# Token rows gathered as quarter rows and turned by VectorE instead of TensorE in a mixture-of-experts kernel

## The reference

```python
v = rms_norm(h, norm2_g).reshape(B * S, D)
h = h + moe(v, router_w, router_b, w1, b1, w2, b2).reshape(B, S, D)
# moe: logits = xf @ router_w + router_b; top_val, top_idx = lax.top_k(logits, 4) of 32 experts
#      gates = softmax(top_val)
def clamped_swiglu_expert(xb, w1, b1, w2, b2):        # for each expert, its tokens only
    h = xb @ w1 + b1                                  # 1024 -> 2 * 1024
    x_glu = jnp.minimum(h[..., :D_FF], 7.0)
    x_lin = jnp.clip(h[..., D_FF:], -7.0, 7.0)
    act = x_glu * jax.nn.sigmoid(1.702 * x_glu) * (x_lin + 1.0)
    return act @ w2 + b2                              # 1024 -> 1024, times the gate, added to the token's row
```

## Time and profile before

| | |
|---|---|
| median of 3 runs | 2027.03 us (2025.29 to 2027.17) |
| the profiled execution's own time | 2026.22 us |
| its span in the trace | 2024.4 us |
| mean granted TensorE clock | 0.985 of full speed |
| PE busy | 1956.3 us, 97% of the span |
| DVE busy | 992.1 us, 49% |
| POOL busy | 228.0 us, 11% |
| HBM traffic | 251 GB/s over the span |

### The profile page before, as it was taken

The page is one execution under the profiler, slowest core; times in us unless marked ns, Lnnn a source line. Parts: engine busy times, 40 slices in busy tenths (PEclk is TensorE's granted clock), DMA queues, the critical chain, the costliest instruction groups (busy, mean ns, idle before and its releaser), DMA issues.

```text
span 2024.4 us, 35446 instructions
## 1 busy us (share of the span) xinstructions
PE 1956.3 (97%) x13245; PEld 1620.3 (80%) x13246; DVE 992.1 (49%) x2418; ACT 451.5 (22%) x983; POOL 228.0 (11%) x221
## 2 busy tenths in 40 slices
PE   6999989969999999999999999999999999999996
PEld 3555544437888877888887888999999999999996
DVE  3998963354455545454454555444444433343332
ACT  3166564111111111111111111221222211111111
POOL 3111100010101100110100010111111111100100
PEclk9999989989999999999999999999999999999998
DMA  6000123537999999998999998998888888887651
GB/s 238 1 1 1 46 59 139 175 131 276 346 321 330 345 334 344 345 335 317 345 334 344 343 339 309 311 315 299 295 295 298 296 301 298 289 284 245 217 174 43
DMA packets 233939, 509.08 MB, mean 251 GB/s; under 512 B 7997, under 2 KB 12633, under 8 KB 233888
## 3 DMA queue, kind: packets, MB, share of 16 engines
q1 hardware_dynamic: 215264, 447.97, 61.2%
q0 software_dynamic: 16768, 59.98, 11.1%
q10 hardware_dynamic: 1856, 0.41, 0.1%
HBM read 475.53 MB, written 32.80 MB: 251 GB/s over the span
## 4 chain that ended last, share of the span: by engine, by line
PE 93%; DVE 3%; ACT 1%; issue 1%; POOL 1%; DMA 0%; SPq 0%; ACTq 0%; DVEq 0%; POOLq 0%
PE bank L1133 49%; PE bank L1173 12%; PE bank L1148 11%; PE bank L1366 6%; PE bank L1244 5%; PE bank L1513 2%; PE bank L1280 2%; DVE arena L874 2%; PE bank L1291 1%; PE bank L1317 1%; PE bank L1161 1%; PE bank L1504 1%; PE bank L1162 1%; DMA arena<-in_x 0%; PE bank L1340 0%
## 5 line engine op out<-in xcount | busy, mean ns | idle before, releaser
L1133 PE MATMUL bank<-arena 128*128 128x128 f32 (+5 forms) x8192 | 993.6, 283 | 6.9 <-DVE arena L1099 5.6
L1133 PEld LDWEIGHTS bank<-arena 128*128 128x128 f32 x8192 | 984.5, 191 | 18.3 <-issue 9.3
L769 DVE TENSOR_SCALAR arena<-bank,b1c 128x256 f32<-128x256 f32 x256 | 123.6, 483 | 424.3 <-PE bank L1133 424.3
L469 ACT ACTIVATE arena<-arena 128x256 f32<-128x256 f32 x256 | 106.6, 417 | 853.3 <-DVE arena L769 853.3
L1099 DVE TENSOR_SCALAR arena<-bank,cols 128x256 f32<-128x256 f32 x256 | 112.0, 479 | 337.0 <-PE bank L1513 337.0
L1173 PE MATMUL bank<-arena 128*128 128x512 f32 x576 | 262.1, 593 | 0.0
L1148 PE MATMUL bank<-arena 128*128 128x144 f32 (+4 forms) x1792 | 246.0, 293 | 0.0
L1148 PEld LDWEIGHTS bank<-arena 128*128 128x128 f32 x1792 | 235.9, 190 | 0.1
L357 POOL DMA_INDIRECT out<-arena,idx_cur x64 | 99.0, 1547 | 873.3 <-DVE arena L817 863.6
L874 DVE SCALAR_TENSOR_TENSOR arena<-arena,cols 128x512 f32<-128x512 f32 (+1 forms) x226 | 182.2, 806 | 16.3 <-ACT arena L562 9.4
L1173 PEld LDWEIGHTS bank<-arena 128*128 128x128 f32 x576 | 102.5, 190 | 94.7 <-issue 94.7
(11 more groups left out here) (226 smaller groups left out, 1107.9 us busy)
## 6 DMA issues: line engine op xcount, KB each, us to landing
arena<-in_w SPq DMA_DIRECT2D x192, 2048.0 KB, 11.4
arena<-in_b SPq DMA_DIRECT2D x32, 512.0 KB, 11.0
arena<-in_x SPq DMA_DIRECT2D x16, 512.0 KB, 6.2
token_rows<-arena SPq DMA_DIRECT2D x8, 528.0 KB, 2.9
out<-arena SPq DMA_DIRECT2D x8, 512.0 KB, 5.9
arena<-in_w_in SPq DMA_DIRECT2D x2, 1536.0 KB, 13.7
arena<-in_w_in SPq DMA_DIRECT2D x1, 3072.0 KB, 20.1
arena<-in_w_out SPq DMA_DIRECT2D x1, 2048.0 KB, 8.2
```

The costliest lines, as they stand in the source:

```text
L469: a.activation(sg[:, m % 2, :], g1[:, m % 2, :], ACT.Sigmoid, scale=ALPHA).then_inc(sg_ready, 1)
L769: v.tensor_scalar(g1[:, r, :], bank[r][:, 0:SLOTS], b1c[:, m:m + 1], LIMIT, ALU.add, ALU.min).then_inc(g1_ready, 1)
L1133: last = mm(bank[m % 2][:, side * SLOTS:side * SLOTS + n], w1_sb[:, k, lo:lo + P], xT[:, k, 0:n], start=k == 0, stop=k == KD - 1)
```

## The change

The gathered data no longer comes as whole rows. `token_rows` holds rows with the gain already multiplied in and with their values in another order: the four quarters of each 128-value block are collected, so that quarter q of a row is 256 contiguous values. POOL gathers eight lists of 128 quarter rows (1 KB each): list g brings tokens 32g to 32g+31, with quarter q of them on partitions 32q to 32q+31. A VectorE transpose of 32x32 blocks then writes 32 columns of `xT` directly. The gates have an HBM scratch of their own and two gathers of 128-byte rows. The indices of the eight lists need one more small matmul (`spots` spread over the partitions by `copies`). `slots_to_tokens` moves from behind group 3 to behind group 2. The first pass still goes by two gathers and PE transposes, with a reordering copy on ACT ahead. The end of the router loop is written in another order too.

```diff
-        def gather(pool, n):
-            pool.wait_ge(idx_ready, n)
+        def gather_gates(pool):
+            for h in range(2):
+                pool.indirect_dma_start(out=gsel[:, h, :], out_offset=None, in_=gates_d,
...
+        def gather_quads(pool, n):
+            pool.wait_ge(idx_q_ready, n)
+            pool.sem_inc(pool_past, 1)
+            for g in range(8):
+                pool.indirect_dma_start(out=gath_q[:, g, :], out_offset=None, in_=quads_d,
+                                        in_offset=bass.IndirectOffsetOnAxis(ap=idx_q[:, g:g + 1], axis=0)
+                                        ).then_inc(quad_in, 16)
...
                 pool.wait_ge(cur_ready, q + 1)
-                pool.wait_ge(xt_mm, q * 4 + 4)
-                gather(pool, q + 2)
+                pool.wait_ge(xt_ev, q * 4 + 4)
+                gather_quads(pool, q + 1)
+                gather_gates(pool)
                 pool.wait_ge(y_ready, q + 1)
...
-                if m == 4:
                     v.wait_ge(idx_mm, q + 2)
-                    first, second = take_idx()
-                    link(first)
-                    second().then_inc(idx_ready, 1)
+                    link(take_codes(v))
+                    link(take_idx(v, idxf[:]))
+                    v.tensor_copy(idx_next[:], idxf[:]).then_inc(idx_ready, 1)
+                    v.tensor_tensor(spots[:], idxf[:].unsqueeze(2).to_broadcast([P, 2, 4]),
+                                    quad[:].unsqueeze(1).to_broadcast([P, 2, 4]), ALU.mult).then_inc(spots_ready, 1)
+                if m == 5:
+                    v.wait_ge(spread_mm, q + 1)
+                    v.tensor_scalar(idx_q[:], bank[6][:, 16:24], 4.0, quad_id[:], ALU.mult, ALU.add
+                                    ).then_inc(idx_q_ready, 1)
             hidden_b(MT - 1)
-            q4 = v.snap(q * 4 + 4)
-            for i in range(4):
-                take_xT(q4, i)
+            v.wait_ge(quad_in, q * 128 + 128)
+            for g in range(8):
+                ins = v.transpose(xT[:, :, g * 32:(g + 1) * 32], gath_q[:, g, :].rearrange("p (k r) -> p k r", k=KD))
+                if g % 2 == 1:
+                    ins.then_inc(xt_ev, 1)
...
             def norm_v(t):
-                v.tensor_scalar(vrow[:, t % 2, 0:D], hb[:, t % 4, :], rs[:, 2, t:t + 1], None, ALU.mult)
+                for g in range(4):
+                    v.scalar_tensor_tensor(dst[:, g], src[:, g], rs[:, 2, t:t + 1], gain[:, g], ALU.mult, ALU.mult)
...
+            residual(NT - 1, (0,))
+            route(NT - 2)
+            residual(NT - 1, (1,))
+            v.wait_ge(lt_mm, NT - 1)
+            v.wait_ge(vt_mm, 2 * NT)
+            v.tensor_copy(vT[:, 4:8, :], bank[5][:].rearrange("p (k q) -> p k q", k=4)).then_inc(vt_ev, 1)
+            norm_v(NT - 1)
+            route(NT - 1)
...
-                        if m == 0 and side == 0 and k % 2 == 0:
-                            pe.wait_ge(xt_ev, q4 - 3 + k // 2)
+                        if m == 0 and side == 0 and k == 0:
+                            pe.wait_ge(xt_ev, q4)
...
-                if m == 3:
+                if m == 2:
                     slots_to_tokens(q + 2)
+                if m == 4:
+                    pe.wait_ge(spots_ready, q + 1)
+                    mm(bank[6][:, 16:24], copies[:], spots[:].rearrange("p h g -> p (h g)"), start=True,
+                       stop=True).then_inc(spread_mm, 1)
...
             if n == P:
-                down_rows(0, range(4))
-                for h in range(2):
-                    pe.wait_ge(gath_in[h], q16 + 16)
-                pe.wait_ge(idx_ready, q + 2)
-                trans_x(q4, 0, halves)
...
+                down_rows(0, range(MT))
+                down_rows(1, range(MT))
                 return
```

More of the change, by code:

```diff
@@ L179, in hybrid_block @@
         gate_cur = sb("gate_cur", [P, 2])
+        gsel = sb("gsel", [P, 2, NE])
+        idxf = sb("idxf", [P, 2])
+        spots = sb("spots", [P, 2, 4])
+        idx_q = sb("idx_q", [P, 8], i32)
+        copies = sb("copies", [P, P])
+        quad = sb("quad", [P, 4])
+        quad_id = sb("quad_id", [P, 1])
         lnv = sb("lnv", [P, 2, NT // 2])
@@ L689, in h_square, with take_vT @@
                              ).then_inc(h_sq, 1)
-            def take_vT(t):
+            def take_vT(t, sides=(0, 1)):
                 if t >= 1:
                     a.wait_ge(lt_mm, t)
-                for b in range(2):
+                for b in sides:
                     a.wait_ge(vt_mm, 2 * t + b + 1)
@@ L725, in _ @@
             take_lT(NT - 1)
[L726 to L729 removed]
             gate_exp(NT - 1)
+            a.wait_ge(h_sq, NT)
+            for h in range(2):
+                a.wait_ge(gath_in[h], 16)
+                a.activation(first_tok[:, h, :].rearrange("p (k q r) -> p q k r", k=KD, q=4),
+                             gath[:, h, :].rearrange("p (q k r) -> p q k r", k=KD, q=4), ACT.Copy
+                             ).then_inc(first_tok_ready, 1)
             for i in range(2):
@@ L955, in _, with residual @@
             softmax_a(NT - 1)
-            def residual(t):
+            def residual(t, sides=(0, 1)):
                 v.wait_ge(xh_in[t % 2], 16 * (t // 2 + 1))
@@ L1346, in weigh_v, with out_half @@
                 last.then_inc(o_mm, 1)
-            def out_half(t, part_, sides=(0, 1)):
+            def out_half(t, part_, sides=(0, 1), ins=range(CT)):
                 if part_ == 0:
@@ L1362, in out_half @@
                 for b in sides:
-                    for i in range(CT):
+                    for i in ins:
                         src = (aT if part_ == 0 else cT)[:, i, t * P:(t + 1) * P]
@@ new lines, in turn_rows @@
+            def turn_rows(u, sides=(0, 1)):
+                if u == 0:
+                    pe.wait_ge(cn_done, 2 * CT)
+                if u == 1:
+                    pe.wait_ge(o_ev, NT)
+                for b in sides:
+                    if u >= 1:
+                        pe.wait_ge(vt_ev, 2 * u)
+                    pe.wait_ge(h_ready if b else h_half, u + 1)
+                    for k in range(4):
+                        c = 4 * b + k
+                        last = pe.transpose(bank[4 + b][:, k * P:(k + 1) * P], hb[:, u % 4, c * P:(c + 1) * P], ident[:])
+                    last.then_inc(vt_mm, 1)
@@ new lines, in logits @@
+            def logits(u):
+                pe.wait_ge(vt_ev, 2 * u + 2)
+                if u >= 1:
+                    pe.wait_ge(lg_neg, u)
+                for j in range(2):
+                    for g in range(4):
+                        last = mm(bank[6][g * NE:(g + 1) * NE, 0:P], rw[:, 4 * j + g, :], vT[:, 4 * j + g, :],
+                                  start=j == 0, stop=j == 1)
+                last.then_inc(lt_mm, 1)
+            for t in range(NT - 1):
+                if t >= 2:
+                    out_half(t, 0)
+                if t >= 1:
+                    turn_rows(t - 1)
+                if t >= 2:
+                    fold_logits(t - 2)
+                if t == 0:
+                    pe.wait_ge(mix_ready, CT)
+                if t == NT // 2:
+                    pe.wait_ge(mix_ready, 2 * CT)
+                out_half(t, 1)
@@ L1469, in _ @@
                     out_half(1, 0, (1,))
-                if 1 <= t <= NT:
-                    u = t - 1
-                    pe.wait_ge(vt_ev, 2 * u + 2)
-                    if u >= 1:
-                        pe.wait_ge(lg_neg, u)
-                    for j in range(2):
-                        for g in range(4):
-                            last = mm(bank[6][g * NE:(g + 1) * NE, 0:P], rw[:, 4 * j + g, :], vT[:, 4 * j + g, :],
-                                      start=j == 0, stop=j == 1)
-                    last.then_inc(lt_mm, 1)
+                else:
+                    logits(t - 1)
                 if t == 1:
@@ L1482, in _ @@
                     weigh_v(NT - 1)
+            out_half(NT - 1, 0)
+            turn_rows(NT - 2)
+            fold_logits(NT - 3)
+            out_half(NT - 1, 1, (0,))
+            logits(NT - 2)
+            out_half(NT - 1, 1, (1,), range(2))
+            turn_rows(NT - 1, (0,))
+            fold_logits(NT - 2)
+            out_half(NT - 1, 1, (1,), range(2, CT))
+            turn_rows(NT - 1, (1,))
+            logits(NT - 1)
             fold_logits(NT - 1)
@@ L1506, in slots_to_tokens @@
                 last.then_inc(idx_mm, 1)
-            def trans_x(before, i, halves=2):
-                if i >= 1:
-                    pe.wait_ge(xt_ev, before + i)
-                for k in (2 * i, 2 * i + 1):
-                    for h in range(halves):
-                        last = pe.transpose(bank[6][:, (k % 2) * SLOTS + h * P:(k % 2) * SLOTS + (h + 1) * P],
-                                            gath[:, h, k * P:(k + 1) * P], ident[:])
-                last.then_inc(xt_mm, 1)
             slots_to_tokens(1)
@@ L1545, in _, with passes @@
                 lap8 = pe.snap(lap * len(WIDTHS))
```

(6 more changed lines are left out.)

169 lines of the change are left out of this document (63 added, 106 removed).

## The result

| | before | changed kernel |
|---|---|---|
| median | 2027.1 us (4 runs) | 2114.97 us (4 runs, 2114.11 to 2118.71) |
| ratio | | 1.0437 [1.0422, 1.0452] |
| span of the profiled execution | 2024.4 us | 2113.1 us |
| mean granted TensorE clock | 0.985 | 0.966 |

The change makes the kernel 88 us slower, where 25 us less were forecast.

The account below looks back on a forecast made before the run. PE was taken as the bound, busy 97% of the span and holding 93% of the chain. 2026.2 - 41.4 + 4.5 + 4.2 + 2.5 + 5 = 2001.0; with the runs' median 0.8 higher, 2001.8 us, range 1992 to 2032.

Parts of the forecast that it names:

- Wide passes: No wait: Wide passes: the next tokens' chain takes 21.3 us where 25 us are left, so PE does not wait.
- rival 1: Narrow passes: tokens come late, 2.0 us a pass (2031 us), 2068 with slow transposes; chance 0.18 beyond break-even, with rival 4.
- Transposes on PE: PE's own path in all passes: 376 row transposes of 0.11 us each go, -41.4 us.
- The spread matmul: Added on PE, once in each of 32 passes: 0.14 us each, +4.5 us, bounds 1.6 to 7.
- The wait for the one-hots: Behind group 2 of the 18 narrow passes: PE waits 0.23 us each, +4.2 us.
- The next tokens in narrow passes: At the end of narrow passes: PE waits 0.3 us for the next tokens in 17 passes, +5 us.
- The last list landed: Next tokens, narrow pass: the eighth list was forecast to land 5.8 us from issue, range 4.4 to 7.5.
- the eight transposes: VectorE, behind the last list's landing: eight transposes at a pitch of 0.42 us, 3.4 us together.
- The estimate of 0.62: One VectorE transpose: 622 ns from the skill page's 311 ns, eight 5.0 us, which would put the sum 27 us higher.
- The router loop: Ahead of the pass loop: the last block's routing starts late, at 438.1, +2.5 us.
- Rival 3: DMA becomes the bound in narrow passes: 2037 us at 0.11 us a packet; chance 0.03.
- Rival 4: VectorE holds up POOL's issues: lists 1.7 us later, wait 2.0 a pass, 2031 us; chance 0.18 together with rival 1.

Follow-up runs that it names:

- experiment 16: The changed kernel with one semaphore count-up on POOL between its eighth list and its gates, nothing else: 2019.46 us, 0.9967.
- 13: The changed kernel with one-hots behind the first group's evictions and one semaphore count-up on POOL between the eighth list and the gates: 2011.82 us, 0.9926.
- experiment 8: The kernel before with eight plain loads per pass by SP, the same bytes as eight extra gathers: 2026.68 us, 1.0002.
- experiments 12 to 14: Changed kernel, one-hots early, plus before the gates a wait with count-up (2008.32 us) or count-up alone (2011.82), or a count-up between the gates' two gathers (2009.64).
- 10 to 15 and 18: Changed kernel, one-hots early, with gates gathered first (10, 11, 15) or a wait or count-up among the last issues (12 to 14, 18): 2008.32 to 2011.82 us.
- experiment 2: The changed kernel with DVE's one-hots written behind the first group's evictions instead of the second's: 2107.87 us, 1.0403.

## Why the prediction was wrong, step by step

- **The step that failed** is "Wide passes: No wait", and with it rival 1's remark that ten issues in a row have no precedent, which it priced only as a late landing. The lists did land in time. What came was a mechanism that neither the sum nor a rival has: the ten issues in a row held ACT, which PE needs for the next column group. By the last column of the table against the second it cost 90.0 us in 13 wide passes, 2.8 in passes 1 to 18, 1.8 in the last and 1.1 behind it: 95.6 of span, 95.5 by the medians (2114.97 - 2019.46). In the pass shown, 5.80 us of idle PE stand against 0.23 in the timeline of 16, and the slow clock takes 2.0 on the first 16 records (4.21 for 2.23), 0.8 on the next 16 and 0.2 on the transposes between: 8.5 in all, as the pass is longer by.
- **Transposes on PE**, -41.4: removed as forecast, but not all of it was won. The chain of one wide pass of experiment 16:

```profile
1478.23 3.69 PE bank L1202 x30
1481.92 0.02 issue
1481.94 0.39 ACT arena L506
1482.34 0.04 issue
1482.38 2.23 PE bank L1202 x16
...
1496.20 0.41 issue
1496.61 8.47 PE bank L1183 x67
```

  In the earlier trace rows a step of four transposes stood where PE now waits 0.45 us for ACT's eviction, and another (0.44) where 0.41 us of issue stand before the next pass, 0.07 before. So of 1.76 us a pass come back 0.45, 0.34 and 0.12 of spread: 0.85 is left to win, and 0.73 was won (13 wide passes: 692.7 to 683.2). Forecast was 1.62, so this term was 11.5 us too large. Work on PE's chain that covers a wait is not won in full when it goes.
- **The spread matmul**, 0.14: 0.12 in the chain. **The wait for the one-hots**, 0.23: too small. The chain of a narrow pass of the changed kernel:

```profile
911.43 0.17 DVE arena L1080
...
911.63 1.47 DVE arena L1080 x7
913.10 0.05 issue
913.15 0.55 PE bank L1543 x16
913.70 7.25 PE bank L1182 x64
920.95 0.12 PE bank L1190 x2
921.08 10.82 PE bank L1182 x96
931.90 13.73 PE bank L1226 x32
```

  Three groups last 10.82 (96 records), so from 901.92 they are done at 912.74 and PE waits 0.41. Experiments 16 and 13 differ in the place of the one-hots alone: a narrow pass in which PE waits for nothing else takes 43.44 us in 16 and 43.03 in 13, 0.41 too. The second product is 13.73, forecast 13.8.
- **The next tokens in narrow passes**, +5: smaller. From the first matmul of the second product to the next pass's first, PE needs 13.74 where it waits for nothing; what passes 1 to 17 of experiment 16 take beyond that adds up to 1.9 us, 0.11 a pass and not 0.3 (in the changed kernel 3.1 us). So the one-hots were 0.18 too low and the tokens 0.19 too high, and the sum for a narrow pass (0.88 - 0.14 - 0.23 - 0.3 = 0.21) came out near the 0.09 that passes 1 to 17 of experiment 16 won each: that is luck. The 18th won 1.1 where 1.39 was forecast, so passes 1 to 18 won 2.7 where the sum has 5.0. Issues stand 1.25 apart. The chain into the second pass of the changed kernel:

```profile
499.76 6.21 DMA arena<-token_rows,idx_q
...
505.99 0.05 DVE arena L854
...
506.36 2.37 DVE arena L854 x7
508.74 0.04 issue
508.78 3.28 PE bank L1182 x27
```

  The last list landed 6.21 us from issue (5.8), and the eight transposes took 2.75 (3.4). One is 0.408 us by the page, near the row that the sum took. The estimate of 0.62 from the Trainium skill's figure ("VectorE: DVE Perf Modes", The three transpose paths) was too high.
- **The router loop**, +2.5: 461.1 to 463.8, +2.7; `438.68 0.18 DVE lg L1032` in the chain is the routing, forecast at 438.1.
- **Rival 3**, DMA as the bound, fell by experiment 8: 1.08 MB more in each pass cost nothing. **Rival 4**, VectorE locks POOL out: in the wide pass shown issues were 0.94 to 1.19 us, the long one where `L818` and `L821` ran, and in the whole trace at most 1.23; at most 0.29 for one issue, not 0.42 for four. The row that the prediction read for this has the issue begun 0.15 us before `L778`, so it couldn't show what an issue suffers that begins behind such an operation, as the one of 1.19 us did. The trap that the Trainium skill names ("SBUF — State Buffer", "DVE blocks DMA") may be in that 0.29; the loss isn't it, since in experiments 12 to 14 VectorE does the same work beside the same issues.
- **Behind the last issue**, 4.9 us more (3.8 in experiment 16), not forecast and not explained.

With the sum's own terms corrected by what experiment 16 shows (11.5 in the 13 wide passes, 3.8 behind the last issue, 2.3 in passes 1 to 18) 2001.8 becomes 2019.4; experiment 16 measured 2019.5. The router loop and the last pass would move that by less than 1. The other 95.5 us are the hold.

## What to carry to other kernels

Where a change puts many indirect DMAs one behind another on GpSimd, look at what the *other* engines do while they are issued, and put a count-up or a wait between them; it is free to try, and here it was worth 4.5 per cent. With it and with early one-hots the change is 0.8 per cent faster than before (2008 to 2012 us in seven kernels that can't be told apart, 10 to 15 and 18). When an engine waits for a "remote" releaser though its inputs are there, compare the end of the wait with the other queues' issues over many passes: a constant distance points at the culprit, and taking it away or breaking it up shows whether it is. And a control that changes the time without changing the work (a busy GpSimd, plain loads of the same bytes) is worth more than a tenth variant of the fix.

## What was not expected of the hardware

- Ten indirect DMAs of 128 rows in a row in GpSimd's queue can hold ACT, DVE or PE until 1.7 to 2.3 us after the end of the last issue. In the two wide passes shown the engine stood from some 7 us (DVE) and 9 us (ACT, PE) after the first issue. Nine in a row and one, eight and two, two and eight, or ten with waits among them hold nobody, at the same pitch of 1.25 us. It was seen in two different kernels (`L505` and `L777`, `L1157`).
- The run of ten is not enough by itself: in the 18 narrow passes of the changed kernel it holds nobody, and in experiment 2 ACT in 12 of 18. Which passes are hit, why ten, and by what path, no run shows.
- A wait instruction isn't needed to break the run: `sem_inc` on a semaphore that nobody waits for took 96 us off (2107.87 to 2011.82).
- A VectorE transpose of 32x32 blocks over 128x256 float32 takes 0.41 us (mean of 256), eight in a row 2.73.
